# A decoder layer on one core: the first pass of the output projection takes eight chunks instead of six

## The reference

```python
hn = rms_norm(x, attn_norm[i])
mix, xq = stick_breaking_mixer(hn, sb_w_in[j])          # 16 heads of 64
cross = cross_attention(xq, mem, ...)                   # 4 heads of 64, 256 memory tokens
x = x + jnp.concatenate([mix, cross], axis=-1) @ w_out[i]   # 1280 x 1024
x = x + swiglu(rms_norm(x, ffn_norm[i]), w_gate[i], w_up[i], w_down[i])
```

## Time and profile before

| | |
|---|---|
| median of 3 runs | 1347.37 us (1347.23 to 1350.07) |
| the profiled execution's own time | 1348.03 us |
| its span | 1346.2 us |
| PE busy | 1324.2 us, 98% |
| DVE busy | 1038.0 us, 77% |
| ACT busy | 685.3 us, 51% |
| POOL busy | 419.0 us, 31% |
| chain that ended last | PE 91%, DVE 4%, ACT 2%, POOL 1% |
| granted clock of TensorE in steps 5 to 7 and the projection | 1.00 |

### The profile page before, as it was taken

The page is one execution under the profiler, slowest core; times in us unless marked ns, Lnnn a source line. Parts: engine busy times, 40 slices in busy tenths (PEclk is TensorE's granted clock), DMA queues, the critical chain, the costliest instruction groups (busy, mean ns, idle before and its releaser), DMA issues.

```text
span 1346.2 us, 20597 instructions
## 1 busy us (share of the span) xinstructions
PE 1324.2 (98%) x6854; PEld 1089.8 (81%) x6854; DVE 1038.0 (77%) x1222; ACT 685.3 (51%) x1202; POOL 419.0 (31%) x309
## 2 busy tenths in 40 slices
PE   7999999999999999999999999999999999999999
PEld 4877888888888887778888788888888888888887
DVE  6677889897988889986348877878777787877866
ACT  7667666666676766773245334343333334333341
POOL 1000000000000000313115855647455484654721
PEclk9999999999999999999999999999999999999999
DMA  6100101001000101203301221211212112121113
GB/s 250 32 24 17 32 25 32 24 23 31 23 23 23 39 16 48 102 17 117 102 17 55 63 71 48 64 58 39 68 39 76 56 39 70 31 74 56 50 32 125
DMA packets 91477, 71.76 MB, mean 53 GB/s; under 512 B 4256, under 2 KB 75936, under 8 KB 91424
## 3 DMA queue, kind: packets, MB, share of 16 engines
q1 hardware_dynamic: 91424, 71.07, 16.9%
HBM read 65.03 MB, written 4.19 MB: 51 GB/s over the span
## 4 chain that ended last, share of the span: by engine, by line
PE 91%; DVE 4%; ACT 2%; POOL 1%; issue 1%; DMA 0%; SPq 0%; ACTq 0%; DVEq 0%; POOLq 0%
PE ps L1363 27%; PE ps L341 17%; PE ps L1538 14%; PE ps L1069 7%; PE ps L395 5%; PE ps L379 5%; PE ps L369 4%; PE ps L1148 3%; PE ps L310 3%; PE ps L1593 2%; PE ps L849 1%; PE ps L789 1%; DVE succ L568 1%; PE ps L992 1%; PE ps L1021 1%
## 5 line engine op out<-in xcount | busy, mean ns | idle before, releaser
L1548 DVE TENSOR_TENSOR x<-ps,x 128x2048 f32<-128x2048 f32 x70 | 160.3, 2290 | 92.7 <-PE ps L1538 92.6
L588 POOL TENSOR_TENSOR o_t<-o_t,pv_low 128x256 f32 x24 | 22.7, 946 | 470.6 <-ACT o_t L481 470.6
L1331 DVE TENSOR_TENSOR part_l<-part_x,part_h 128x512 fp32r<-128x512 f32 x140 | 141.7, 1036 | 25.3 <-POOL part_x L1309 17.8
L1526 POOL TENSOR_TENSOR bl<-bx_B,bh 128x512 fp32r<-128x512 f32 x70 | 93.1, 1330 | 208.9 <-ACT bh L1522 208.9
L341 PE MATMUL ps<-hh,w_h 128*128 128x512 f32 x336 | 140.6, 419 | 0.0
L469 ACT ACTIVATE a_h<-ps 128x256 fp32r<-128x256 f32 (+2 forms) x96 | 78.0, 812 | 121.4 <-PE ps L379 120.7
L341 PE MATMUL ps<-hh,w_l 128*128 128x512 f32 x336 | 132.1, 393 | 0.0
L341 PE MATMUL ps<-hl,w_h 128*128 128x512 f32 x336 | 131.5, 391 | 0.0
L1363 PE MATMUL ps<-ft_h,part_h 128*128 128x512 f32 x320 | 124.6, 389 | 0.0
L1363 PE MATMUL ps<-ft_l,part_h 128*128 128x512 f32 x320 | 124.6, 389 | 0.0
L1363 PE MATMUL ps<-ft_h,part_l 128*128 128x512 f32 x320 | 124.6, 389 | 0.0
(11 more groups left out here) (286 smaller groups left out, 3412.5 us busy)
## 6 DMA issues: line engine op xcount, KB each, us to landing
w_raw<-in_sb_w_in SPq DMA_DIRECT2D x52, 256.0 KB, 2.9
bx_B<-in_w_down SPq DMA_DIRECT2D x44, 256.0 KB, 3.0
part_x<-in_w_gate SPq DMA_DIRECT2D x40, 256.0 KB, 2.9
part_x<-in_w_up SPq DMA_DIRECT2D x40, 256.0 KB, 2.9
wo_raw<-in_w_out SPq DMA_DIRECT2D x20, 256.0 KB, 2.8
x_in<-in_x SPq DMA_DIRECT2D x8, 512.0 KB, 7.1
x<-in_x SPq DMA_DIRECT2D x16, 256.0 KB, 5.9
out<-x SPq DMA_DIRECT2D x16, 256.0 KB, 2.0
```

Of the source, the lines that this page charges most:

```text
L1331: dve.tensor_tensor(part_l[m][p][:, :, :].rearrange(flat), part_x[m][p][:, :, :].rearrange(flat), part_h[p][:, :, :].rearrange(flat).bitca ...
L1526: pool.tensor_tensor(bl[(par + k) % 2][:, :], bx[B_OPS[k]][:, :], bh[(par + k) % 2][:, :].bitcast(F32), ALU.subtract).then_inc(s_bw, 1)
L1548: dve.tensor_tensor(o, ps[:, 0:4], o, ALU.add).then_inc(s_x2, 1)
```

## The change

The first pass now takes chunks 0 to 5, 8 and 9 and the second chunks 6 and 7. So 48 matmuls (8 pieces by 2 chunks by 3) move from behind step 7 into it, and `FILL` deals them out anew: 9, 9, 6, 24, 12, 12, 24, 24, 24, 24, 12, 12 matmuls for units 0 to 11, where it was 9, 9, 9, 9, 18, 9, 9, 18, 9, 9, 18, 18. Three of the nine of unit 0 stand before T(0). The early halves leave units 1, 4, 5, 8, 9, 10 and 11 of step 6 and go to units 5 and 11 of steps 4, 5 and 6, which is why steps 4 and 5 are taken out of the loop. In unit 11 their low halves stand ahead of `dve_v`. The weights of chunks 4 and 5 are split by ACT at the end of step 6 (`PRE_END`), ahead of step 7's first `act_fail`, and POOL makes their low halves ahead of its last heads of step 6. SP loads all residual rows after the last piece of `w_out`.

```diff
-        EX = [("o", k, 0) for k in range(6)] + [("o", 0, 1)]
+        EX = [("o", k, 0) for k in (8, 0, 1, 2, 3, 4, 5)]
...
                     if u == 0:
+                        pe_project(pe, 0, some=(0,))
                         pe_transposes(pe, s, u)
...
             act_low_rows(act, s, NU - 1)
+            if isinstance(s, int) and s == PAIRS - 2:
+                for i in PRE_END:
+                    act_split(act, i)
...
-        def dve_open(dve, s, par):
+        def dve_open(dve, s, par, between=()):
             dve_scan(dve, s, 1, 0)
             dve_scan(dve, s, 1, 1)
             dve_weights(dve, s, 1)
+            for i in between:
+                split_low(dve, i)
             dve_v(dve, par, TUSE * s)
...
-        EARLY = 6
-        LATE_ORDER = (8, 9, 6, 7)
-        PRE_AT = {1: [EX[0]], 4: [EX[1]], 5: [EX[2]], 8: [EX[3]], 9: [EX[4]],
-                  10: [("w", 0, 0), ("w", 1, 0), EX[5]], 11: [("w", 2, 0), ("w", 3, 0), EX[6]]}
-        SPLITS = [("w", k, 0) for k in range(4, EARLY)] + [("o", k, 1) for k in range(1, EARLY)]
-        SPLITS += [i for k in LATE_ORDER for i in (("w", k, 0), ("o", k, 0))]
+        EARLY_ORDER = (0, 1, 2, 3, 4, 5, 8, 9)
+        LATE_ORDER = (6, 7)
+        PEELED = PAIRS - 4
+        PRE_AT = {(PEELED, 5): [EX[0]], (PEELED, NU - 1): [EX[1], EX[2]],
+                  (PEELED + 1, 5): [EX[3]], (PEELED + 1, NU - 1): [EX[4]],
+                  (PEELED + 2, 5): [EX[5]], (PEELED + 2, NU - 2): [("w", 0, 0), ("w", 1, 0)],
+                  (PEELED + 2, NU - 1): [EX[6], ("w", 2, 0), ("w", 3, 0)]}
+        PRE_END = [("w", 4, 0), ("w", 5, 0)]
+        SPLITS = [("w", 8, 0), ("o", 9, 0), ("w", 9, 0)] + [("o", k, 1) for k in EARLY_ORDER]
+        SPLITS += [("w", k, 0) for k in LATE_ORDER] + [("o", k, 0) for k in LATE_ORDER]
...
-        SPLIT_RATE = (2, 1, 1, 1, 1, 1, 1, 1, 2, 2, 2, 0)
-        DVE_RATE = (0, 0, 1, 1, 1, 1, 1, 0, 1, 1, 1, 1)
+        SPLIT_RATE = (3, 1, 1, 2, 1, 1, 2, 0, 1, 1, 2, 0)
+        DVE_RATE = (1, 1, 1, 1, 2, 1, 1, 1, 0, 0, 0, 2)
...
-                if N == OC + 4:
-
-                    sp.wait_ge(s_o, 4 * PAIRS + 1)
-                    sp.wait_ge(s_op, NT)
-                    sp.wait_ge(s_mvd, 16 * len(EX))
-                    for t in range(NT):
-                        sp.dma_start(x2_row(t)[:, 0:BANK], xd[:, t, 0:BANK]).then_inc(s_x2l[0][t], 16)
...
+            sp.wait_ge(s_o, 4 * PAIRS + 1)
+            sp.wait_ge(s_op, NT)
+            sp.wait_ge(s_mvd, 16 * len(EX))
             for t in range(NT):
-                sp.dma_start(x2_row(t)[:, BANK:D], xd[:, t, BANK:D]).then_inc(s_x2l[1][t], 16)
+                for side in range(2):
+                    c = slice(side * BANK, (side + 1) * BANK)
+                    sp.dma_start(x2_row(t)[:, c], xd[:, t, c]).then_inc(s_x2l[side][t], 16)
```

More of the change, by code:

```diff
@@ L497, in act_step @@
                 act_high(act, s, u)
-                if isinstance(s, int) and s == PAIRS - 2:
-                    for i in PRE_AT.get(u, ()):
+                if isinstance(s, int):
+                    for i in PRE_AT.get((s, u), ()):
                         act_split(act, i)
@@ L594, in dve_open, with early_halves @@
             dve_weights(dve, s, 1)
+            for i in between:
+                split_low(dve, i)
             dve_v(dve, par, TUSE * s)
+        def early_halves(s, u):
+            return [i for i in PRE_AT.get((s, u), ()) if i[0] == "o"] if isinstance(s, int) else []
         def dve_step(dve, s, par, last=False):
@@ L611, in dve_step @@
                     dve_weights(dve, *nxt)
-                if isinstance(s, int) and s == PAIRS - 2:
-                    for i in PRE_AT.get(u, ()):
-                        if LOW[i][0] == 1:
-                            split_low(dve, i)
+                if u < NU - 1:
+                    for i in early_halves(s, u):
+                        split_low(dve, i)
                 if last:
@@ L619, in dve_step @@
             if not last:
-                dve_open(dve, s + 1, 1 - par)
+                dve_open(dve, s + 1, 1 - par, early_halves(s, NU - 1))
         s_last = sem("last_tile_weights_done")
@@ L693, in trunk @@
         CU = XP * NT
[L695 to L704 removed]
+        EARLY_ORDER = (0, 1, 2, 3, 4, 5, 8, 9)
+        LATE_ORDER = (6, 7)
+        LAST_ORDER = EARLY_ORDER + LATE_ORDER
+        EARLY = len(EARLY_ORDER)
+        PEELED = PAIRS - 4
[4 more added lines that the diff above has]
+        PRE_END = [("w", 4, 0), ("w", 5, 0)]
+        PRE = [i for at_ in sorted(PRE_AT) for i in PRE_AT[at_]] + PRE_END
+        SPLITS = [("w", 8, 0), ("o", 9, 0), ("w", 9, 0)] + [("o", k, 1) for k in EARLY_ORDER]
+        SPLITS += [("w", k, 0) for k in LATE_ORDER] + [("o", k, 0) for k in LATE_ORDER]
         LATER = [("o", k, 1) for k in LATE_ORDER]
[L706 removed]
+        SECOND = [("w", k, 1) for k in LAST_ORDER]
         HIGH = {i: n + 1 for n, i in enumerate(PRE + SPLITS + LATER + SECOND)}
@@ L873, in act_split @@
             if i in PRE and what == "o":
-                act.wait_ge(s_o, 4 * (k + 1) + 1)
+                if k < PAIRS:
+                    act.wait_ge(s_o, 4 * (k + 1) + 1)
+                else:
+                    act.wait_ge(s_co, CU)
             if what == "o" and k >= PAIRS - 2 and k < PAIRS:
@@ L1050, in pe_project @@
             last = i == 3 * NT - 1
-            order = (range(EARLY), LATE_ORDER, LAST_ORDER if last else range(OC))[i // NT]
+            order = (EARLY_ORDER, LATE_ORDER, LAST_ORDER)[i // NT]
             if i == ALONE:
@@ L1749, in trunk @@
         block = ctx.enter_context(nc.Block())
-        LOOPS = (PAIRS - 2) // 2
+        LOOPS = (PAIRS - 4) // 2
         @block.sync
@@ L1772, in _ @@
                         load_w(sp, 2 * m + par + 1, k)
-            for k in range(6):
-                load_w(sp, PAIRS - 1, k)
+            for s in range(PEELED + 1, PAIRS):
+                for k in range(6):
+                    load_w(sp, s, k)
             sp.wait_ge(s_wl, W1)
@@ L1836, in _ @@
                         pool_heads(pool, 2 * m + par, u)
+            for s in range(PEELED, PAIRS - 2):
+                for u in GROUP_END:
+                    pool_heads(pool, s, u)
             for u in GROUP_END:
@@ L1944, in _ @@
                     act_step(act, 2 * m + par, par)
-            act_step(act, PAIRS - 2, 0)
+            for s in range(PEELED, PAIRS - 1):
+                act_step(act, s, s % 2)
             act_step(act, PAIRS - 1, 1, last=True)
@@ L2075, in _ @@
                     dve_step(dve, 2 * m + par, par)
-            dve_step(dve, PAIRS - 2, 0)
+            for s in range(PEELED, PAIRS - 1):
+                dve_step(dve, s, s % 2)
             dve_step(dve, PAIRS - 1, 1, last=True)
@@ L2197, in _ @@
                     pe_step(pe, 2 * m + par, par)
-            pe_step(pe, PAIRS - 2, 0)
+            for s in range(PEELED, PAIRS - 1):
+                pe_step(pe, s, s % 2)
             pe_step(pe, PAIRS - 1, 1, last=True)
```

16 lines of the change are left out of this document (7 added, 9 removed).

## The result

The change makes the kernel slower: 1353.62 us (median of 6 runs, 1352.30 to 1354.50) against 1348.13 (median of 6 runs of the kernel before in the same session), a ratio of 1.0041 [1.0030, 1.0051], some 5.5 us. The profiled execution took 1353.88, its span 1352.1, against 1348.03 and 1346.2. The direction was forecast, the size was not: 1351.5 was predicted for the median, with 1353.5 as the upper end.

The account below looks back on a forecast made before the run. TensorE, busy 98% of the span, was taken as the bound, so only its work or waits count. Terms +0.4 - 1.1 + 4.2 + 0.9 - 3.4 + 0.1 + 0.9 + 2.15 gave +4.1 us, 1351.5; range 1347.0 to 1353.5.

Parts of the forecast that it names:

- T(11): Tail of step 7: unit 10 falls from 18 matmuls to 12, so TensorE waits for VectorE's product: +0.9 us (to 1.5).
- steps 4 and 5: Early halves in unit 5 make T(7) wait 0.2 us a step, those in unit 11 cost nothing: +0.4 us (0 to +0.8).
- step 6: The wait at T(3) goes and that at T(7) falls from 0.54 to 0.2: -1.1 us (at most -1.8).
- start of step 7: VectorE's low half of chunk 9 waits for ScalarE's high half, delaying scans and T(3): +4.2 us (+2.4 to +5.6).
- V(5) and T(6): Unit 4 of step 7: two low halves on VectorE make V(5) and the product of unit 6 late: +0.9 us (0.3 to 1.2).
- old waits of step 7: Units 6 to 9 get 24 matmuls each, more than any of their waits, so five old waits go: -3.4 us.
- copy race: Units 6 to 9: a piece waits for the copy of the one before, behind only one group of transposes: +0.1 us.
- second pass: Pieces fall from 12 matmuls to 6; piece 9 waits for a copy, piece 10 for VectorE's low halves: +2.15 us (1.5 to 2.4).
- SP's rows: Residual rows issued after the last pieces of w_out, at about 646 to 654 us: costed at nothing.
- Not slower: Rival: VectorE reaches T(3) of step 7 at 569.9 as before, so the 4.2 is gone: 1347.3 us; chance 0.22.
- Faster: Rival: T(3) as before, and the last units and second pass take no new waits: -4.0, 1343.3 us; chance 0.08.
- Slower still: Rival: POOL and VectorE exclude each other fully in the first units, T(11) met as before: 1353.5 us; chance 0.14.

Follow-up runs that it names:

- kept_busy: The changed kernel with twelve matmuls added to the filler of unit 1, where TensorE waits before V(1): 1351.87 us, ratio 1.0031 to the kernel before.
- low_later: The changed kernel with VectorE's low half of chunk 9 moved from unit 0 to unit 1, behind the product of unit 2: 1351.62 us against 1347.53, ratio 1.0027.
- half_first: The changed kernel with ScalarE making the high half of chunk 9 ahead of weight 8's: 1351.69 us, ratio 1.0027 to the kernel before.
- unit_eleven: The changed kernel with the early halves of unit 5 in steps 4 to 6 moved to unit 11: 1353.29 us, ratio 1.0041 to the kernel before.
- unit_ten_copy: The changed kernel with six matmuls of piece 6 moved from unit 9 to 10 and ScalarE's copy of that piece one unit later: 1351.80 us against 1348.13, ratio 1.0029.
- rows_early: The changed kernel with the left halves of the residual rows loaded where the kernel before did: 1358.57 us against 1347.07, ratio 1.0085.
- no_meeting: The changed kernel with GpSimd writing zeros for the low halves of weights 8 and 9 instead of computing them: 1352.21 us against 1348.13, ratio 1.0029.
- seven_chunks: The changed kernel with mends to its queues and filler, and chunk 9 back in the second pass: 1346.30 us against the kernel before's 1348.13, ratio 0.9982.
- seven_again: The mended kernel with seven chunks in the first pass, unchanged, run once more for a second profile: 1345.39 us.

## Why the prediction was right and wrong

**Direction and mechanism: right.** V(1) waits for the a_l behind the low half, which waits for `o_h`, and the waits at V(5), T(11), piece 9 and piece 10 are where they were forecast. By the terms of the sum, with 0.16 us added to an idle time as the prediction does:

| term | forecast | measured |
|---|---|---|
| steps 4 and 5 | +0.4 | +0.6 |
| step 6 | -1.1 | -0.6 |
| start of step 7, at full clock (kept_busy) | +4.2 | +4.6 |
| V(5) and T(6) | +0.9 | +0.8 |
| old waits of step 7 | -3.4 | -3.4 |
| copy race | +0.1 | 0 |
| T(11) | +0.9 | +0.9 |
| second pass | +2.15 | +2.0 |
| lower clock (after against kept_busy) | none | +1.0 |
| stretch ahead of step 0 (-0.2) and what is not accounted for (+0.2) | none | 0 |
| sum | +4.1 | +5.9 |

**Start of step 7.** T(3) is 4.0 us later than before, 4.7 with the three matmuls fewer. At full clock it would be hardly earlier: by kept_busy 0.1, which leaves 4.6 for the term. The trace of after alone suggests more, because VectorE ended the product at 573.07 and TensorE, slow by then, reached T(3) only at 573.77; but the slow TensorE had also moved GpSimd's heads out of that product's way.

That 4.2 came out so near is in part luck. VectorE's low half took 1.69 where I had 0.6, so in spite of an `o_h` that came 0.4 earlier than computed, counted from `dve_v` (561.63 to 562.27), the scans of unit 2 started 6.62 after `dve_v` where I had 6.02. From there to the end of the product of unit 3 it took 9.15 where I had 10.1: GpSimd was through with its weights when the product of unit 2 came (0.94), and an old idle time of 0.38 behind it went. Before the change that product ran beside GpSimd:

```profile
563.78 1.38 DVE L568 TENSOR_TENSOR succ<-fail,succ 128x768 f32<-128x768 f32 x1
```

These are two errors of opposite sign. My reason for taking the middle, that the old stretch had meetings as well, is borne out: one went from the product of unit 2 when the late half got one. low_later and half_first show that no single order mends it: without ScalarE's wait the same low halves run into GpSimd, and T(3) is still 1.8 and 2.9 us later than before.

**The step that failed: the sum had no term for TensorE's clock.** I took the long wait as its own length. Behind it TensorE ran some 7 us at a granted clock of 0.50. The price varies between executions: from `dve_v` of step 7 to the end of the projection it took 148.53 with no fall (kept_busy, with its added work hidden in the wait), 149.52 in after, and 150.35 in unit_eleven, whose step 7 is that of after and where the clock fell at about 565.9 and came back at about 576.1. So it is 1.0 us in the profile of after and 1.8 in the other, most of it behind T(3), whose eight transposes take 1.56 in after and 0.84 in kept_busy. All six runs of after had a mean clock of 0.996 or 0.997. The rest of the miss is of sizes: 0.7 in steps 4 to 6 and 0.4 at the start of step 7. Without the clock's 1.0 the loss would be 4.9 us, inside the sum's bounds of +2.3 to +5.5.

The runs of unit_ten_copy show the clock without any trace: two runs at a mean clock of 1.000 took 1350.19 and 1350.57, four at 0.997 1351.45 to 1351.86, one at 0.996 1352.53, three at 0.995 1353.53 to 1354.74. A fall ahead of step 0 is in these means as well, so they don't price the one fall. This kernel is after without the 0.9 of T(11), so at a clock of 1.000 after would take an estimated 1351.3, against some 1347.2 of the kernel before at 1.000: 4.1 us. By the stretches of kept_busy and the kernel before (1216.8 and 1211.7) it would be 5.1.

**Steps 4 to 6.** -0.7 was forecast, 0.0 measured. Each T(7) costs about 0.2, as forecast. Missed by a size: steps 4 and 5 lost 0.3 each, as T(8) comes another 0.1 later, and step 6 gained 0.6 and not 1.1. Its missing 0.5 is at its end, which I had not counted: from T(11) to `dve_v` it takes 8.38 where it took 7.86. A half stood in that stretch before as well. What changed is what GpSimd's low halves of weights 2 and 3 meet there: it was a product and the half (1.00 and 1.78 us), and is now the product and the scans (1.53 and 2.36; these scans took 1.26 before). No run of its own shows this. unit_eleven shows that moving the halves out of unit 5 gives 0.5 over the three steps.

**Rows, second pass, T(11).** The second pass was right to 0.15 us, by the rule that a piece is ready when its matmuls are, but its accumulator is free when an engine comes to it. SP's rows cost nothing where they were put, and rows_early shows that this was not a matter of course: the old place would have cost another 5 us. I had not looked at it as a part of the change.

**Rivals.** "Not slower" falls: T(3) is not before 573. "Faster" falls by the same. "Slower still" had the right time, 1353.5, by the wrong mechanism: GpSimd's meetings are real, but they gave 4.6 for the term and not 5.6, and T(11) was as forecast, not met once more. The rest was the clock and steps 4 to 6. The range ended 0.1 us below the median; it held no wait that costs more than its length.

What stays open: what decides whether the clock falls behind a wait. Behind 1.95 us at T(3) it fell in no_meeting and not in half_first, behind 2.1 us in seven_chunks and not in seven_again; and two of ten runs of unit_ten_copy, whose profile has a wait of 3.58, had a mean clock of 1.000. The Trainium skill, page TensorE: Matmul & The Clock Gate, section Part 1: The HAM clock gate, says that the moment at which the clock rises after a kernel's start differs from run to run of one kernel. The runs here show such a difference for the fall (1.0 and 1.8 us for one code of step 7), and I could not tell more.

## What to carry to other kernels

Work moved into a stage as filler brings its preparation with it: here the matmuls were free where they went, but three of the operands that chunks 8 and 9 needed first (both weights, and the half of chunk 9) were made in the one place where the stage had no slack, and with the same mends seven chunks won where eight lost. Before moving work ahead, walk through the queue of each engine that prepares it, and ask what stands behind an instruction whose operand comes late. Price a long wait of TensorE above its length, since what follows it may run at the lower clock, and look at the granted clock of the windows behind it, because the busy column calls slow matmuls full work. And look at mean clocks of the runs before trusting a difference of 1 to 2 us in their medians.
